# Eight start addresses modulo 512 for the tiles of the normalised activations

## The reference, cut to what matters

```
h = x
h = h + 0.5 * swiglu(rmsnorm(h), w_in 1024x5632, w_out 2816x1024)       # first FFN
u = rmsnorm(h); proj = u @ w_in(1024 x 7168)                            # q, k, v, g, p, gates
h = h + (gate0 * (retention(q, k, v) @ w_ret_up) + gate1 * (pool(p) @ w_pool_up)) @ w_out
h = h + 0.5 * swiglu(rmsnorm(h), ...)                                   # second FFN
h = rmsnorm(h)
h = h + 0.5 * swiglu(rmsnorm(h), ...)                                   # third FFN
u = rmsnorm(h) @ w_mix_in(1024 x 3592)                                  # conv and gated delta rule
h = h + concat(short_conv, gated_delta_rule) @ w_mix_out
h = h + 0.5 * swiglu(rmsnorm(h), ...)                                   # fourth FFN
out = rmsnorm(h)
```

## Time and profile before

| what | value |
|---|---|
| median of the runs | 2485.89 us |
| span of the profiled execution | 2485.5 us |
| mean granted TensorE clock | 0.977 of full |
| TensorE matmuls busy | 2353.5 us, 95% |
| VectorE, ScalarE, GpSimd busy | 42%, 29%, 28% |
| DMA | 86 GB/s |

### The profile page before, as it was taken

How to read it: one execution, slowest core, us unless ns; L and a number is a source line. 1 busy time by engine, 2 the same in 40 slices (tenths; PEclk the granted TensorE clock), 3 DMA queues, 4 the chain that set the end, 5 groups by cost and what they waited for, 6 DMA issues and landing times.

```text
span 2485.5 us, 27928 instructions
## 1 busy us (share of the span) xinstructions
PE 2353.5 (95%) x10696; PEld 1928.2 (78%) x10696; DVE 1038.8 (42%) x1127; ACT 726.6 (29%) x922; POOL 688.9 (28%) x489
## 2 busy tenths in 40 slices
PE   6999999899999999999999999997877889999997
PEld 5888888687777788888877888866766778888886
DVE  3444334444344444443444434326544445444323
ACT  4322222232223333322323232224322134322221
POOL 3444204401121014443114445001222212444300
PEclk9999999999999999999999999998988999999999
DMA  3333333233222323333322232331100012333332
GB/s 114 97 97 94 101 102 127 83 104 100 62 68 70 98 86 93 101 93 102 102 89 89 93 101 93 102 97 51 50 28 26 26 43 79 95 98 93 101 102 84
DMA packets 58819, 213.34 MB, mean 86 GB/s; under 512 B 6528, under 2 KB 6784, under 8 KB 58624
## 3 DMA queue, kind: packets, MB, share of 16 engines
q1 hardware_dynamic: 58464, 210.02, 27.2%
q0 software_dynamic: 288, 2.36, 0.3%
HBM read 210.26 MB, written 2.10 MB: 85 GB/s over the span
## 4 chain that ended last, share of the span: by engine, by line
PE 86%; DVE 4%; issue 4%; POOL 3%; ACT 2%; DMA 0%; SPq 0%; POOLq 0%; DVEq 0%
PE acc L457 26%; PE acc L459 26%; PE acc L458 26%; DVE c_acc L1621 1%; PE mixb L688 1%; PE mixb L706 1%; PE mixb L701 1%; PE mixb L846 1%; PE sums L489 1%; POOL p_sum L1734 1%; PE acc L798 1%; ACT w_hi L907 1%; PE acc L799 1%; PE acc L800 1%; POOL p_out L1739 1%
## 5 line engine op out<-in xcount | busy, mean ns | idle before, releaser
L457 PE MATMUL acc<-x_hi,w_hi 128*128 128x512 f32 x2016 | 806.0, 400 | 22.3 <-DMA cst<-const 10.8
L458 PE MATMUL acc<-x_lo,w_hi 128*128 128x512 f32 x2016 | 794.4, 394 | 0.0
L459 PE MATMUL acc<-x_hi,w_lo 128*128 128x512 f32 x2016 | 793.5, 394 | 0.0
L457 PEld LDWEIGHTS acc<-x_hi,w_hi 128*128 128x128 f32 x2016 | 385.0, 191 | 105.3 <-issue 21.8
L459 PEld LDWEIGHTS acc<-x_hi,w_lo 128*128 128x128 f32 x2016 | 384.1, 191 | 82.1
L458 PEld LDWEIGHTS acc<-x_lo,w_hi 128*128 128x128 f32 x2016 | 385.2, 191 | 77.1
L1218 DVE TENSOR_TENSOR w_lo<-w_raw,w_hi 128x1024 fp32r<-128x1024 f32 x232 | 300.2, 1298 | 287.9 <-ACT w_hi L907 287.2
L1293 DVE TENSOR_TENSOR w_lo<-w_raw,w_hi 128x1024 fp32r<-128x1024 f32 x160 | 244.8, 1530 | 271.1 <-ACT w_hi L913 271.1
L907 ACT ACTIVATE w_hi<-w_raw 128x1024 fp32r<-128x1024 f32 x232 | 242.5, 1051 | 222.4 <-DMA w_raw<-weights 222.4
L459 PE MATMUL acc<-hid_hi,w_lo 128*128 128x512 f32 x704 | 280.9, 399 | 0.0
L458 PE MATMUL acc<-hid_lo,w_hi 128*128 128x512 f32 x704 | 277.4, 394 | 0.0
(11 more groups left out here) (309 smaller groups left out, 2065.8 us busy)
## 6 DMA issues: line engine op xcount, KB each, us to landing
w_raw<-weights SPq DMA_DIRECT2D x392, 512.0 KB, 3.5
h<-x_t SPq DMA_DIRECT2D x4, 512.0 KB, 8.4
y_t<-h SPq DMA_DIRECT2D x8, 256.0 KB, 2.1
k1c<-const POOLq DMA_DIRECT2D x1, 1536.0 KB, 8.3
k2c<-const POOLq DMA_DIRECT2D x1, 768.0 KB, 6.5
cst<-const SPq DMA_DIRECT2D x1, 161.0 KB, 7.6
vec<-vectors SPq DMA_DIRECT2D x1, 112.5 KB, 3.5
```

The lines of the kernel that those rows point to most:

```text
L457: pe.matmul(bank, w_hi[:, slot, w], hi, start=start, stop=False)
L458: pe.matmul(bank, w_hi[:, slot, w], lo, start=False, stop=False)
L459: return pe.matmul(bank, w_lo[:, slot, w], hi, start=False, stop=stop)
```

## The change

Each tile of `x_hi` and of `x_lo` gets some columns of padding behind it, 16 for `x_hi` and 20 for `x_lo`. The views named `x_hi` and `x_lo` have the same shape as before, and no instruction is added or taken away. The offset behind `x_lo` is rounded up to a multiple of 512.

```diff
         at = 0
         h, at = sbuf_at("h", at, [KD, S])
-        x_hi, at = sbuf_at("x_hi", at, [KD, S], F32R)
-        x_lo, at = sbuf_at("x_lo", at, [KD, S], F32R)
+        x_hi_rows, at = sbuf_at("x_hi", at, [KD, S + 16], F32R)
+        x_lo_rows, at = sbuf_at("x_lo", at, [KD, S + 20], F32R)
+        x_hi, x_lo = x_hi_rows[:, :, 0:S], x_lo_rows[:, :, 0:S]
+        at = (at + 511) // 512 * 512
         w_raw, _ = sbuf_at("w_raw", at, [SLOTS, TILES * P])
```

## The result

The changed kernel took 2503.45 us (median of four runs, 2493.19 to 2503.88) against 2485.99 us before. The ratio is 1.006, 95% interval 1.0048 to 1.0072. Measured again with five runs it was 2501.26 us against 2485.74 us, ratio 1.0066 (1.0052 to 1.0079). By the medians it is slower by 17.5 us and 15.5 us, as forecast in its direction, and by about half of the forecast 32.5 us.

A forecast was written before the change was run, and what follows sets the result against it. TensorE's matmul count times the distance between starts was taken as the bound. Terms of 29.6 + 1.8 + 1.1 = 32.5 us on a span of 2485.5 gave 2518 us, with a range from 2482 to 2545.

The forecast's parts named there:

- What bounds the kernel: Whole kernel: TensorE matmuls busy 95% of the span, so only a changed distance between matmul starts can matter.
- Step 1, the mechanism: Matmuls streaming `x`: staggered tiles leave no eight matmuls at one common place, so the 226.7 ns distance is lost.
- settled state: Streamed matmuls: the 226.7 ns distance that tiles with one common place modulo 512 reach after about eight matmuls.
- Step 1, the size: 6048 matmuls streaming `x`: +5.5 ns each, 29.6 us plus 1.8 us in the second mixer; ends -16 and +62 us.
- first case: Matmuls with `x`: settled state lost, chance 0.52, time 2518 us, range 2507 to 2545.
- The half of the mixer's share: Second mixer, 672 matmuls streaming `x`: half of +5.5 ns each counted, the rest falling into existing waits; 1.8 us.
- Step 2: v projection, 192 matmuls with `x` loaded as stationary operand: +5.5 ns each, 1.1 us, between 0 and 2.
- Step 3: Writing the `x` tiles on VectorE and ScalarE: no effect from the new addresses, 0, with 2 us either way.
- Step 4: Everything behind `x_lo`: weights stay at 0 and `arena` at 352 modulo 512, `hid` and `mix` keep 233.3 ns: 0.
- The tile that pays alone: Rival: only tiles starting between multiples of 64 pay, 1512 `x_lo` matmuls at 6.6 ns, +10 us, 2496 us; chance 0.13.
- The irrelevant place: Rival: place modulo 512 doesn't matter, `x` keeps 226.7 ns and time is 2486 us; no-effect chance 0.20.
- different places keep reads apart: Rival: shifting streamed `x` tiles against the weight loads removes collisions, -2.7 ns per matmul, -16 us, 2470 us; chance 0.15.

The follow-up runs named there:

- second profile: The changed kernel profiled and run once more without any edit: 2501.26 us, with a span of 2503.3 us in the profiled execution.
- w64: Kernel before, with the weights moved to 64 modulo 512 and `x` and `arena` at 0: 2515.9 us.
- all64: Kernel before, with `x`, weights and `arena` all moved to 64 modulo 512: 2468.3 us.
- lo32: Kernel before, with only the `x_lo` tiles at 32 modulo 512 and `x_hi`, weights and `arena` at 0: 2494.3 us.
- arena0: Kernel before, with `arena` (`hid` and others) moved from 352 to 0 modulo 512, `x` untouched: 2467.43 us, ratio 0.9933.
- x64_arena32: Kernel before, with every `x` tile at 64 and `arena` at 32 modulo 512, weights at 0: 2500.3 us.
- hi256step: Kernel before, with 64 columns of padding per `x_hi` tile, so its tiles alternate between 0 and 256 modulo 512: 2487.5 us, ratio 1.0002.
- lo64: Changed kernel, with `x_lo` padded by 16 columns instead of 20, so all `x` tiles start at multiples of 64: 2505.7 us.

## Why the prediction was half right

*What bounds the kernel* held: 95% TensorE before and after, and the change of time lies where `x` is read. The `x` halves of the FFNs bring 14.6 of the 17.8 us between the second profile and the kernel before.

*Step 1, the mechanism*, held. The settled state with 226.7 ns belongs to a relation between the streamed tile and the weights, and the change takes it away. `w64` and `all64` show the relation, `lo32` the memory from tile to tile, `arena0` that `hid` lost its 6.6 ns by it. The uneven distances and the 5.53 us for 24 starts (forecast 5.55 to 5.60) are the sign that the prediction named, a little short of its size. The wording "one common place" missed the condition: a place that all tiles of `x` share is not enough (`x64_arena32`) and not needed (`hi256step`); each tile's place has to be that of the weights, modulo 256.

*Step 1, the size*, is the step that failed: the term of +5.5 ns for each matmul with `x` streamed. I took +5.5 ns, between the unsettled stretch (+4.6) and `hid` (+6.6), and the runs show 230.4 - 226.7 = +3.7 ns, below both. With 3.7 the same term is 5376 x 3.7 = 19.9 us in place of 29.6. The reason that I gave for going up from 4.6, the `x_lo` tiles off a multiple of 64, is refuted by `lo64`. And to treat the changed stream as a lasting transient was wrong: it has a mean of its own, the same in both profiles. The `x` halves of the four FFNs grew by 3.5 to 3.8 us each, and I had given their long stretches about 6. The lower end of the first case didn't follow from its words either: +4.6 ns in 6048 matmuls is 28 us, and with half of it hidden the time would be 2500 and not 2507. The medians (2501 and 2503) lie in between. Why the mean is 3.7 longer and not 5 stays open.

*The half of the mixer's share* (1.8 us): +1.0 measured, where two executions of one kernel differ by 8.6, so it isn't told. In the heads and gates +2.5 us were measured for 40 blocks, 960 matmuls; at 3.7 ns they should bring 3.6. I had counted nothing as hidden there.

*Step 2*, 1.1 us for the v projection: +0.2 in the second profile, +1.5 in the first. The distances show that the term was right. At full clock 24 starts with the weights streamed and `x` loaded took 5.44 us before (first rows) and 5.58 us in the second profile (second rows), 226.7 and 232.5 ns:

```profile
479.08 0.39 PE L800 MATMUL acc<-w_lo,x_hi 128*128 128x512 f32 x1
...
484.52 0.39 PE L800 MATMUL acc<-w_lo,x_hi 128*128 128x512 f32 x1
```

```profile
480.42 0.40 PE L802 MATMUL acc<-w_lo,x_hi 128*128 128x512 f32 x1
...
486.00 0.39 PE L802 MATMUL acc<-w_lo,x_hi 128*128 128x512 f32 x1
```

So the relation counts with the roles exchanged too. The stage hides it: a pause of TensorE in it was 5.80 us in the second profile and 6.38 before, and in the first profile 12 of its distances ran at half the granted clock (1.2 GHz), where before and in the second profile it was 6.

*Step 3*, nothing from the writes: held. *Step 4*, `hid` unchanged: held.

*The rivals.* The tile that pays alone falls by `lo32` and `lo64`, though its 10 us were nearer to the measured 15 to 17 than mine. The irrelevant place falls by `arena0`. That different places keep reads apart falls in the form stated: none of the eleven layouts has a mean under 226.7 ns.

*The page that spoke against it.* The Trainium skill, "SBUF — State Buffer", section "Who interferes with whom", lets TensorE wait for no other engine. No run here contradicts that. But the Trainium skill, "TensorE: Matmul & The Clock Gate", section "Step-by-step: what each phase is for", also says that loading the next weights takes no read bandwidth from the running matmul. For these float32r matmuls the runs disagree in effect: moving the weights alone by 64 bytes takes the distance from 226.7 ns to 233.3 (`w64` against `arena0`). Whether it is read bandwidth that is lost, no run shows.

**What stays open.** Why the mean is 230.4 for the change, 231.7 for `lo64`, and 228.8 or 233.3 for a constant 64, and which of the last two is taken. That the two reads collide in the memory is the obvious reading of `w64` and `all64`, but it was only argued: the runs show the relation of the addresses and not what happens at them.

## What to carry to other kernels

Where TensorE bounds a float32r kernel, read the distance between starts for each streamed tensor from the timeline, and not the busy time; two values for the same shape at full clock are a reason to compare the start addresses of the streamed tiles and the weights. Put the streamed tiles and the weights on the same place modulo 256 bytes: in this kernel one rounded offset was worth 18 us of 2486. Check a padding that is meant to spread accesses by the same distances, since one displaced tensor slows its neighbours in the stream as well.

## What the runs showed that I had not expected

- The favoured relation repeats every 256 bytes: `x` at 256 ran at 226.7 ns, `hid` at 128 at 233.3.
- One stream of `x` at one constant place had two lasting means in one execution, 233.3 and 228.8 ns.
- The second mixer took 397.0 and 405.6 us in two profiles of one kernel, with a mean granted clock of 0.92 and 0.90.
